# Softmax attentions in another order, with a spare 512-column product per query in some stretches

## The chip, the core and the metric

The kernel runs on one NeuronCore of one Trainium2 chip. The metric is the device time of one execution in microseconds (us). The core has a matrix engine (TensorE, PE in the profile, with its weight loads as PEld), a vector engine (DVE), an activation engine (ACT), GpSimd (POOL) and a queue engine (SP). Each engine runs its own instructions strictly in the order in which they were written, and waits at semaphores for the others. TensorE is granted one of two clocks, 2.4 GHz (1.00 in the profile's PEclk) and 1.2 GHz (0.50).

## What is computed

A first block (four kinds of sequence mixing, depth 1) is followed by a second block of two layers. What matters here are the softmax attentions: one forgetting attention in the first block, and in each layer of the second a differential attention (two softmaxes per query block, the second subtracted with a weight) and a neighbourhood attention (one softmax with a bias).

```python
def forgetting_attention(q, k, v, log_f):
        logits = (jnp.einsum('bhqd,bhkd->bhqk', qb, k) * scale
                  + cb[..., None] - cum[:, :, None, :])
        logits = jnp.where(key_pos[None, :] <= q_pos[:, None], logits, -jnp.inf)
        return jnp.einsum('bhqk,bhkd->bhqd', jax.nn.softmax(logits, axis=-1), v)
...
def diff_core(q, k, v, lam):
    s = jnp.einsum('bhcqd,bhckd->bhcqk', q, k).astype(jnp.float32) * (DIFF_QK ** -0.5)
    a = jax.nn.softmax(s, axis=-1)
    w = (a[:, :, 0] - lam * a[:, :, 1]).astype(v.dtype)
    return jnp.einsum('bhqk,bhkd->bhqd', w, v)
...
        s_loc = jnp.einsum('bhjd,bhajkd->bhjak', qr, kr).astype(jnp.float32) * scale + bias
        s_ctx = jnp.einsum('bhjd,bhcd->bhjc', qr, kc).astype(jnp.float32) * scale
        s = jnp.concatenate([s_loc.reshape(b, N_NA, GRID_W, n_loc), s_ctx], axis=-1)
        a = jax.nn.softmax(s, axis=-1).astype(vr.dtype)
```

## The kernel before

All five attentions run through one function, `softmax_attention` (L601). It takes a list of queries (a query is one head with one block of 128 positions) and writes, for each engine, a loop over t = 0 .. n + 1. The queries are software-pipelined through that loop. The steps of query t are these.

- **scores** (PE, L640): products of the query with its keys into PSUM, 128 x `kw`. In the differential attention there are two (n_comp = 2), c0 and c1, with 32 contraction rows each; `score_tile` gives two PSUM slots in turn, so scores of one component wait (`exped`) for the exponential of the one two before.
- **maximum** (DVE, L686): one per component, after the score; the neighbourhood attention adds its bias first (L685).
- **exponential** (ACT, L725): one per component, after its maximum.
- **combine** (DVE, `combine`): for two components a reciprocal (L695), a ratio (L696) and the weighted sum (L699); for one only a reciprocal (L693). It waits for all exponentials of the query.
- **turn** (PE, L653): `kw`/128 transposes of the weights; it waits for combine (or, with one component, for the exponential).
- **copy** (ACT, L733, `copy_turned`): the transposed weights to SBUF; ACT does it behind the exponentials of the next query.
- **mix** (PE, L663): `kw`/128 products with the values. **output** (DVE, L704): the result scaled into `y`.

In turn t of the loop, before the change, PE does scores(t), the work beside, turn(t-1), mix(t-2). DVE does combine(t-1), the maxima of t, output(t-2), the work beside. ACT does the exponentials of t, copy(t-1), the work beside.

The work beside is handed in as functions (`pe_beside`, `dve_beside`, `act_beside`). In the forgetting attention (16 queries, `kw` 128 to 512) it is part of the modulation's products. In the differential attention it is first the projection of six weight units of 128 x 1024 (`n_pieces` pieces, each 24 products at L228 to L230), then normalisation jobs (one 128 x 128 product with up to 512 columns each at L1834, square, root and scale around it), then nothing. Layer 0 has 24 queries: 0 to 15 with `kw` 768, 16 to 23 with `kw` 256; pieces run beside 0 to 11 and jobs beside 12 to 19. Layer 1 has 16 queries, all with `kw` 768; pieces run beside 0 to 7, jobs beside 8 to 13. A weight unit is split into a high part by ACT (L420, called from `act_beside`, so behind copy(t-1)) and a low part by DVE (L428); PE waits for the low part. In layer 1, the pieces 4 to 7 each use a unit of their own, which was split in the turn before. In the neighbourhood attention (24 and 16 queries) the work beside is a Fourier transform (kinds "features", L2094, and "tokens", L2100), a gate and transposes.

The differential attention flows from the work before it without a meeting of engines, and ends in one (`meet`); the neighbourhood attention lies between two.

## Time and profile before

| | us |
|---|---|
| median of 3 runs | 2380.97 (2379.16 to 2387.37) |
| the profiled execution | 2386.32 |
| its span in the trace | 2384.5 |
| matmul busy (PE) | 2247.4 |
| VectorE busy (DVE) | 1237.9 |
| ScalarE busy (ACT) | 752.4 |
| forgetting attention, from and to (span's clock) | 369 to 436 |
| differential attention, layer 0 | 693 to 841 |
| neighbourhood attention, layer 0 | 841 to 958 |
| differential attention, layer 1 | 1725 to 1850 |
| neighbourhood attention, layer 1 | 1850 to 1940 |

The page gives busy times per engine and, in 40 slices, the clock that TensorE was granted. A timeline row is: start, duration, engine, line, operation, what it writes and reads, shapes, how many were merged, and in brackets how long the engine stood idle before it and who released it. One fp32 product is recorded as two matmuls (halves). Busy times include the end of the pipeline, so two PE rows may overlap by some tenths of a microsecond.

### The profile page before, as it was taken

To read this page: it belongs to the slowest core of one execution; us is meant where nothing else is said; L and a number is where in the kernel's file an instruction comes from. 1 tells how busy PE (TensorE), PEld (TensorE's weight loads), DVE (VectorE), ACT (ScalarE), POOL (GpSimd) and SP (SyncE) were. 2 spreads that over 40 slices of the span, in tenths; PEclk is the share of its full clock that TensorE was granted. 3 is DMA by queue.
4 is the path that set the end of the run, shared out by engine and by line. 5 is a ranking of instruction groups with operands and counts; after the bars stand their busy time and mean duration, and the time that the engine had idled before them with its cause. 6 is when DMAs were issued, how large, how long until landed. Compare 5 with 4: busy or idle time off the path is not lost.

```text
span 2384.5 us, 29921 instructions
## 1 busy us (share of the span) xinstructions
PE 2247.4 (94%) x11458; PEld 1758.2 (74%) x11458; DVE 1237.9 (52%) x1923; ACT 752.4 (32%) x1154; POOL 42.3 (2%) x75
## 2 busy tenths in 40 slices
PE   6999899999999999989999989998999999999898
PEld 5678785456778657778888878886777676888786
DVE  5653333347335645466666653436456456666543
ACT  4521112354234523341111112234335333222232
POOL 0001110000000000000000000000000000000000
PEclk9999899899999779999999999999998889999999
DMA  5531216752111200111111111121112002222222
GB/s 185 168 131 38 71 47 221 264 193 71 53 45 36 85 0 1 46 52 62 62 62 62 62 62 62 55 70 53 62 39 90 1 27 80 89 97 96 88 94 74
DMA packets 50397, 187.95 MB, mean 79 GB/s; under 512 B 5424, under 2 KB 5424, under 8 KB 49664
## 3 DMA queue, kind: packets, MB, share of 16 engines
q1 hardware_dynamic: 46688, 168.32, 21.0%
q0 software_dynamic: 2240, 15.48, 1.7%
q10 hardware_dynamic: 1376, 2.85, 0.3%
q8 instruction: 66, 1.08, 0.2%
q14 instruction: 27, 0.22, 0.0%
HBM read 184.53 MB, written 2.10 MB: 78 GB/s over the span
## 4 chain that ended last, share of the span: by engine, by line
PE 85%; DVE 8%; ACT 2%; issue 2%; PEld 1%; DMA 1%; DVEq 0%; ACTq 0%; PEldq 0%; SPq 0%; POOLq 0%
PE psum L228 21%; PE psum L229 20%; PE psum L230 20%; PE psum L640 5%; PE psum L663 5%; PE psum L653 3%; PE psum L2100 2%; PE psum L1736 1%; PE psum L1290 1%; PE psum L1279 1%; PE psum L1301 1%; PE psum L1298 1%; DVE h_low L386 1%; PE psum L1834 1%; DVE unit_low L428 1%
## 5 line engine op out<-in xcount | busy, mean ns | idle before, releaser
L228 PE MATMUL psum<-h_high,unit_high 128*128 128x512 f32 (+1 forms) x1528 | 562.4, 368 | 12.4 <-DVE h_low L386 6.4
L229 PE MATMUL psum<-h_low,unit_high 128*128 128x512 f32 (+1 forms) x1528 | 549.9, 360 | 0.0
L230 PE MATMUL psum<-h_high,unit_low 128*128 128x512 f32 (+1 forms) x1528 | 549.7, 360 | 0.0
L420 ACT CAST unit_high<-ring 128x1024 fp32r<-128x1024 f32 x194 | 203.3, 1048 | 619.9 <-PE psum L230 619.2
L428 DVE TENSOR_TENSOR unit_low<-ring,unit_high 128x1024 fp32r<-128x1024 f32 x194 | 236.9, 1221 | 256.7 <-ACT unit_high L420 256.7
L228 PEld LDWEIGHTS psum<-h_high,unit_high 128*128 128x128 f32 x1528 | 289.3, 189 | 83.4 <-issue 19.5
L230 PEld LDWEIGHTS psum<-h_high,unit_low 128*128 128x128 f32 x1528 | 289.0, 189 | 46.2
L229 PEld LDWEIGHTS psum<-h_low,unit_high 128*128 128x128 f32 x1528 | 289.6, 190 | 41.4 <-issue 0.7
L228 PE MATMUL psum<-hidden_part_high,unit_high 128*128 128x512 f32 (+1 forms) x528 | 190.1, 360 | 19.9 <-DVE hidden_part_low L2365 16.8
L229 PE MATMUL psum<-hidden_part_low,unit_high 128*128 128x512 f32 (+1 forms) x528 | 189.1, 358 | 0.0
L230 PE MATMUL psum<-hidden_part_high,unit_low 128*128 128x512 f32 (+1 forms) x528 | 187.9, 356 | 0.0
L2251 DVE TENSOR_SCALAR conv_out<-psum,parameters 128x512 f32<-128x512 f32 (+1 forms) x132 | 91.2, 718 | 176.9 <-PE psum L230 176.9
L725 ACT ACTIVATE probs<-psum,neg_max 128x768 f32<-128x768 f32 (+4 forms) x136 | 105.6, 780 | 238.5 <-DVE neg_max L686 220.6
L2256 DVE SCALAR_TENSOR_TENSOR conv_out<-psum,parameters,conv_out 128x511 f32<-128x511 f32 (+1 forms) x264 | 166.4, 658 | 23.9 <-DVE conv_out L2251 1.7
L640 PE MATMUL psum<-p 32*128 32x512 f32 (+4 forms) x464 | 142.9, 540 | 3.6 <-ACTq L203 1.8
L704 DVE TENSOR_SCALAR y<-psum,inv 128x64 f32<-128x64 f32 x96 | 27.2, 284 | 203.8 <-PE psum L663 203.8
L663 PE MATMUL psum<-v,turned 128*128 128x64 f32 x912 | 125.7, 289 | 2.3 <-DVE y L704 2.3
L228 PEld LDWEIGHTS psum<-hidden_part_high,unit_high 128*128 128x128 f32 x528 | 100.2, 190 | 36.5 <-issue 16.6
L663 PEld LDWEIGHTS psum<-v,turned 128*128 128x128 f32 x912 | 123.1, 212 | 3.0 <-issue 1.9
L686 DVE TENSOR_REDUCE neg_max<-psum 128x1 f32<-128x768 f32 (+4 forms) x136 | 105.9, 803 | 34.4 <-PE psum L640 33.1
L230 PEld LDWEIGHTS psum<-hidden_part_high,unit_low 128*128 128x128 f32 x528 | 100.2, 190 | 15.6
L229 PEld LDWEIGHTS psum<-hidden_part_low,unit_high 128*128 128x128 f32 x528 | 100.4, 190 | 14.2
(363 smaller groups left out, 2906.4 us busy)
## 6 DMA issues: line engine op xcount, KB each, us to landing
ring<-in_w_units SPq DMA_DIRECT2D x317, 512.0 KB, 3.3
dft<-in_dft POOLq DMA_DIRECT2D x2, 2048.0 KB, 7.9
bias<-in_na_bias POOLq DMA_DIRECT2D x2, 2048.0 KB, 13.0
xT<-in_x ACTq DMA_DIRECT2D x4, 512.0 KB, 6.3
xT<-in_x POOLq DMA_DIRECT2D x1, 2048.0 KB, 11.0
out_x<-xT SPq DMA_DIRECT2D x1, 2048.0 KB, 7.2
constants_first<-in_constants_first POOLq DMA_DIRECT2D x1, 1361.0 KB, 9.1
xT<-in_ctx POOLq DMA_DIRECT2D x1, 1024.0 KB, 15.5
```

Of the source, the lines that this page charges most:

```text
L228: pe.matmul(out, lh, rh, start=first, stop=False, skip_group_check=True)
L229: pe.matmul(out, lh, rl, start=False, stop=False, skip_group_check=True)
L230: return pe.matmul(out, ll, rh, start=False, stop=last, skip_group_check=True)
L420: act.copy(K.w_high[:, q % 2], K.ring[:, q % RING]).then_inc(K.high_split.sem, 1)
L428: dve.tensor_tensor(K.w_low[:, q % 2], K.ring[:, q % RING], K.w_high[:, q % 2].bitcast(F32), ALU.subtract).then_inc(K.unit_used.sem, 1)
L640: mm = pe.matmul(score_tile(t, c, c0, c0 + w), lhs, rhs, start=(g == 0), stop=(g == len(group) - 1), skip_group_check=len(group) > 1)
L653: mm = pe.transpose(K.psum[:, 4 * S + b * P:4 * S + b * P + P], probs[:, t % 2, 0, b * P:b * P + P], const(K, "ident"))
L663: mm = pe.matmul(K.ps[6][:, 0:HD], turned[:, t % 2, b * P:b * P + P], items[t]["v"](tile), start=(b == 0), stop=(b == len(tiles) - 1))
L686: max_ready.up(dve.reduce_max(neg_max[:, t, c:c + 1], score_tile(t, c, 0, kw), AX, negate=True))
L725: exped.up(act.activation(probs[:, t % 2, c, 0:kw], score_tile(t, c, 0, kw), ACT.Exp, bias=neg_max[:, t, c:c + 1], accum_out=row_sum[:, t, ...
L2251: ins = dve.tensor_scalar(t[:, j, c0:c0 + w], bank[:, 0:w], column(wc + 44), column(bc), ALU.mult, ALU.add)
L2256: ins = dve.scalar_tensor_tensor(part, bank[:, src:src + w - 1], column(wc + 88 * (tap - 1)), part, ALU.mult, ALU.add)
```

## The change

Three things change in `softmax_attention`, and two callers pass a new argument.

1. PE does mix(t-2) ahead of turn(t-1) instead of behind it, in all five attentions.
2. With two components, DVE does the maximum of c0 of query t, then combine(t-1), then the maximum of c1 of t. With one component its order stays.
3. A query in the new range `warm` gets one more product on PE, ones (128 x 128) with 512 columns of the constants, fp32, written into its first score tile ahead of the scores and overwritten by them; it stands behind the wait on `exped`. There are 28: queries 12 to 23 of the differential attention of layer 0, 8 to 15 of layer 1, and 0 to 3 of both neighbourhood attentions.

```diff
@@ softmax_attention, tensor engine
                     n = t * n_comp + c
                     if n >= 2:
                         pe.wait_ge(exped.sem, exped.base + n - 1)
+                    if t in warm and c == 0:
+                        pe.matmul(score_tile(t, c, 0, S), const(K, "ones"), K.cst[:, 0:S], start=True, stop=True)
                     for group in items[t]["scores"][c]:
...
                 if beside:
                     beside(pe, t)
+                if 0 <= t - 2 < n_items:
+                    mix(t - 2)
                 if 0 <= t - 1 < n_items:
                     turn(t - 1)
-                if 0 <= t - 2 < n_items:
-                    mix(t - 2)
@@ softmax_attention, vector engine
-            def maxima(t):
+            def maxima(t, comps):
                 kw, bias = items[t]["kw"], items[t]["bias"]
-                for c in range(n_comp):
+                for c in comps:
...
             for t in range(n_items + 2):
+                if t < n_items and n_comp == 2:
+                    maxima(t, range(1))
                 if 0 <= t - 1 < n_items:
                     combine(t - 1)
                 if t < n_items:
-                    maxima(t)
+                    maxima(t, range(n_comp - 1, n_comp))
@@ differential_attention
-    softmax_attention(K, items, K.neg_lam[:, layer:layer + 1], pe_beside, dve_beside, act_beside, end=False)
+    softmax_attention(K, items, K.neg_lam[:, layer:layer + 1], pe_beside, dve_beside, act_beside, end=False,
+                      warm=range(n_pieces, len(items)))
@@ neighbourhood_attention
-    softmax_attention(K, items, None, pe_beside, dve_beside, act_beside)
+    softmax_attention(K, items, None, pe_beside, dve_beside, act_beside, warm=range(4))
```

PE, differential attention of layer 0, around the first two queries with a job (12 and 13); the four products from `p` are the scores, those from `probs` the turn, those from `turned` the mix. Before:

```order
L640 MATMUL psum<-p 128x512
L640 MATMUL psum<-p 128x256
L640 MATMUL psum<-p 128x512
L640 MATMUL psum<-p 128x256
L1834 MATMUL psum<-head_squares,constants 128x512
L653 MATMUL psum<-constants,probs 128x128 x6
L663 MATMUL psum<-v,turned 128x64 x6
```

and now:

```order
L639 MATMUL psum<-constants 128x512
L642 MATMUL psum<-p 128x512
L642 MATMUL psum<-p 128x256
L642 MATMUL psum<-p 128x512
L642 MATMUL psum<-p 128x256
L1838 MATMUL psum<-head_squares,constants 128x512
L665 MATMUL psum<-v,turned 128x64 x6
L655 MATMUL psum<-constants,probs 128x128 x6
```

The spare product stands ahead of the scores, and the mix ahead of the turn. DVE at the same place; the two reductions are the maxima, the sum into `probs` ends the combination. Before:

```order
L695 RECIPROCAL inv<-row_sum 128x2
L696 SCALAR_TENSOR_TENSOR ratio<-inv,row_sum,scalars 128x1
L699 SCALAR_TENSOR_TENSOR probs<-probs,ratio 128x768
L686 TENSOR_REDUCE neg_max<-psum 128x1 x2
L704 TENSOR_SCALAR y<-psum,inv 128x64
L1848 SCALAR_TENSOR_TENSOR p<-p,parameters,head_rstd 128x512
L1827 TENSOR_TENSOR head_squares<-p 128x512
```

and now:

```order
L688 TENSOR_REDUCE neg_max<-psum 128x1
L697 RECIPROCAL inv<-row_sum 128x2
L698 SCALAR_TENSOR_TENSOR ratio<-inv,row_sum,scalars 128x1
L701 SCALAR_TENSOR_TENSOR probs<-probs,ratio 128x768
L688 TENSOR_REDUCE neg_max<-psum 128x1
L706 TENSOR_SCALAR y<-psum,inv 128x64
L1852 SCALAR_TENSOR_TENSOR p<-p,parameters,head_rstd 128x512
L1831 TENSOR_TENSOR head_squares<-p 128x512
```

One maximum moved ahead of the combination, so the combination now stands behind scores(t).

## Rows read from the trace of the kernel before

**Rows 1.** The page: busy time by engine, and the granted clock in 40 slices.
```profile
PE 2247.4 (94%) x11458; PEld 1758.2 (74%) x11458; DVE 1237.9 (52%) x1923; ACT 752.4 (32%) x1154; POOL 42.3 (2%) x75
...
PEclk9999899899999779999999999999998889999999
```

**Rows 2.** Windows (from:to, length, busy by engine, PEclk, DMA): layer 0, jobs and end.
```profile
788.00:842.00 54.00, 47.88 (x217) 33.72 (x216) 34.53 (x89) 29.95 (x78) 0.00 (x0) 0.70 0.14 57
```

**Rows 3.** Timeline, layer 0, differential attention: turn t = 15 at the full clock.
```profile
803.54 1.56 PE L640 MATMUL psum<-p 32*128 32x512 f32 x8
...
804.58 0.16 DVE L695 RECIPROCAL inv<-row_sum 128x2 f32<-128x2 f32 x1
...
805.96 1.82 DVE L686 TENSOR_REDUCE neg_max<-psum 128x1 f32<-128x768 f32 x2
...
806.10 0.88 PE L653 MATMUL psum<-constants,probs 128*128 128x128 f32 x6 [0.36 <-DVE probs L699]
...
806.81 1.45 PE L663 MATMUL psum<-v,turned 128*128 128x64 f32 x12
...
808.19 1.43 PE L640 MATMUL psum<-p 32*128 32x256 f32 x4
```

**Rows 4.** Timeline, same attention: starts of scores 13 and 23, and the last output.
```profile
789.35 1.86 PE L640 MATMUL psum<-p 32*128 32x512 f32 x6
...
833.99 1.41 PE L640 MATMUL psum<-p 32*128 32x256 f32 x4
...
841.01 0.28 DVE L704 TENSOR_SCALAR y<-psum,inv 128x64 f32<-128x64 f32 x1 [1.27 <-PE psum L663]
```

**Rows 5.** Timeline, same attention: a turn with keys of 256 columns (t = 17).
```profile
814.41 0.16 DVE L695 RECIPROCAL inv<-row_sum 128x2 f32<-128x2 f32 x1
...
815.26 0.75 DVE L686 TENSOR_REDUCE neg_max<-psum 128x1 f32<-128x256 f32 x2
...
815.40 0.44 PE L653 MATMUL psum<-constants,probs 128*128 128x128 f32 x2
```

**Rows 6.** Timeline and waits of PE, layer 1, differential attention beside the projection.
```profile
1761.82 0.80 ACT L733 COPY turned<-psum 128x768 f32<-128x768 f32 x1 [3.36 <-PE psum L653]
1762.52 1.05 ACT L420 CAST unit_high<-ring 128x1024 fp32r<-128x1024 f32 x1
...
1763.91 1.22 DVE L428 TENSOR_TENSOR unit_low<-ring,unit_high 128x1024 fp32r<-128x1024 f32 x1
...
PE psum L228 <- DVE unit_low L428: 1.8, 3, 0.6
PE psum L1834 <- DVE head_squares L1827: 1.3, 1, 1.3
```

**Rows 7.** The same spare product elsewhere (all halves: min/median/max), and dense halves in a timeline.
```profile
L354 PE MATMUL psum<-constants x32: 592/592/1061, 568.6 to 1998.9; 128*128 128x512 f32 x32
...
854.52 7.13 PE L2100 MATMUL psum<-dft,fourier_z 128*128 128x512 f32 x16
```

**Rows 8.** Timeline, layer 1, differential attention: scores 9 and 15, a late exponential, the last output.
```profile
1800.05 0.89 ACT L725 ACTIVATE probs<-psum,neg_max 128x768 f32<-128x768 f32 x1
...
1800.35 2.29 PE L640 MATMUL psum<-p 32*128 32x512 f32 x8
...
1833.60 2.94 PE L640 MATMUL psum<-p 32*128 32x512 f32 x8
...
1849.51 0.28 DVE L704 TENSOR_SCALAR y<-psum,inv 128x64 f32<-128x64 f32 x1 [2.98 <-PE psum L663]
```

**Rows 9.** Neighbourhood attention, layer 0: timeline rows, and windows for the clock.
```profile
863.52 1.55 PE L640 MATMUL psum<-p 64*128 64x512 f32 x4
...
871.57 2.07 PE L2094 MATMUL psum<-constants,p 128*128 128x256 f32 x4 [1.95 <-DVE fourier_z L2145]
...
842.00:852.00 10.00, 10.00 (x20) 5.32 (x20) 5.04 (x7) 4.01 (x6) 0.00 (x0) 0.50 0.00 0
871.00:884.00 13.00, 12.43 (x31) 8.10 (x32) 5.50 (x11) 2.78 (x5) 0.00 (x0) 0.50 0.01 1
```

More of the change, by code:

```diff
@@ L601, in softmax_attention @@
 def softmax_attention(K, items, neg_lam=None, beside=None, dve_beside=None, act_beside=None,
-                      end=True):
+                      end=True, warm=range(0)):
     n_comp = len(items[0]["scores"])
```

## Prediction

> **What bounds the kernel now.** I read the page first: TensorE is busy for 94% of the span and VectorE for 52%, and the granted clock is at its upper level but for a few slices [rows 1]. So most of the kernel is matmul at 2.4 GHz and the change doesn't touch it. The slices with a 7 lie in the differential and the neighbourhood attention of layer 0; over the jobs and the end of the differential attention the clock's mean is 0.70 [rows 2]. Then I read the timeline of one turn of the loop, because only there does one see what a swap of two steps is worth.
>
> A turn with 768 keys at the full clock runs so [rows 3]: scores at 803.54, combination from 804.58, turn at 806.10 right behind its last sum, mix at 806.81, next scores at 808.19. TensorE waits only 0.36 us for the combination. The turns are thus nearly full of PE work and still hang on DVE. In the stretch with jobs, from scores 13 at 789.35 to scores 23 at 833.99, ten turns take 44.64 us [rows 4], part of it at 1.2 GHz. Scores 13 to 16 alone take 808.19 - 789.35 = 18.84 us for three turns, though the third takes 4.65 [rows 3, 4].
>
> The profiled execution is 2386.32 us with a span of 2384.5, and lies 5.4 us above the median of 2380.97. I work out differences in the trace and apply them to the median. A measurement of this kernel can tell about 0.3% (7.1 us) from no change.
>
> **Price of one spare product.** The trace has the very product elsewhere, at L354: a half takes 592 ns at its median and 1061 at most, with the end of the pipeline in it [rows 7]. In a dense run 16 halves take 7.13 us, so a half takes some 0.435 us and a product 0.87 us at 2.4 GHz; 1.74 us at 1.2 GHz.
>
> **The new turn, full clock, 768 keys.** PE does spare product, scores, job, mix(t-2), turn(t-1). DVE does the first maximum, the combination, the second maximum. The turn now has a closed chain: spare product 0.87, scores c0 1.55 (a component with nothing beside it, [rows 9]), its maximum 1.82/2 = 0.91, combination to the start of the turn 806.10 - 804.58 = 1.52, transposes 806.81 - 806.10 = 0.71 [rows 3]. Sum 5.56 us. PE's own work in it is 0.87 + 1.56 + 0.65 (a job of 512 or 256 columns) + 1.38 + 0.71 = 5.2, so the chain ends last. Without the spare product the chain would be 4.69, below the 5.2 or so of the old turns at the full clock. So order and product nearly cancel: the order is worth half a microsecond a turn and the product takes it back. What remains depends on the clock.
>
> **Layer 0, jobs.** Turns 13 to 15: 3 x 5.56 = 16.7. Turn 16 has scores of 256 columns and a combination of 768: 0.87 + 0.70 (half of 1.41 at the half clock, [rows 4]) + 0.38 + 1.52 + 0.71 = 4.2. Turn 17 is PE's: 0.87 + 0.70 + 0.65 + 1.38 + 0.24 = 3.85. Turns 18 to 22: 0.87 + 0.70 + 0.38 + 0.99 (814.41 to 815.40) + 0.24 = 3.2 each [rows 5], 16.0. Together 40.7 against 44.64: **-3.9**. From scores 23 to the last output it takes 7.0 now [rows 4]. With the mix done ahead, I count 0.70 + 0.38 + 0.99 + 0.38 + 0.6 + 0.99 + 0.3 + 0.5 + 0.56 = 5.4: **-1.6**. All this takes the full clock for granted. Queries 20 to 23 have no job, and the spare product is most of their dense work; at 1.2 GHz such a turn would be 1.74 + 1.41 + 0.38 + 0.99 + 0.5 = 5.0, thus 1.8 more, 7.2 for four. I take **+2** of 0 to 7, as I expect a fall towards the end.
>
> **Layer 1, jobs.** Scores 9 to 15 took 33.25 for six turns [rows 8]; six at 5.56 are 33.4: **0**. The end, scores 15 to the last output, took 15.9 at the half clock. At the full clock: 1.55 + 0.91 + 1.52 + 0.91 + 1.0 + 1.52 + 0.8 + 0.9 + 1.45 = 10.6, a gain of 5.3; at the half clock 13.8, a gain of 2.1. I take **-4.5**, nearer to the full clock, because the spare products run until scores 15.
>
> **Layer 1, projection: a cost of the new order.** ACT splits the next weight unit behind copy(t-1), and copy(t-1) waits for the turn. Now the copy starts 0.85 us after the turn's start, 1761.82, the cast at 1762.52, the low part at 1763.91, and PE waits for it 3 times, 1.8 us in all [rows 6]. With the mix (1.38) ahead of the turn the copy starts 1.38 later. The low part started 0.34 behind the end of the cast, as DVE had output and copy to do first; that slack is eaten, so it ends 1.38 - 0.34, about 1.05 us later. PE reaches the piece at the same time as before, so each of the three waits grows by that, and so does the wait for the first job's square (1.3 [rows 6]), which stands behind a low part. **+4.3** (bounds 0, if DVE or ACT is ahead, and 5.5, four full mixes). In layer 0 a unit is used two turns later, so some 6 us of piece cover it: 0. The forgetting attention has PE full with the modulation's products: 0, between -0.5 and +0.5.
>
> **Neighbourhood attentions.** Here one component is at work, DVE's order stays, and PE is full from the start: it runs 842 to 852 without a gap, at 1.2 GHz [rows 9]. The spare products 0 and 1 are bare time at 1.74 each, product 2 at 0.87. Product 3 stands before an idle time of 1.95 that DVE ends, and is hidden; if that idle goes, it costs 0.87 more. Two layers: **+8.7**. Against it: denser work may lift the clock earlier. If it rises 3.5 us earlier in each, that is half of 3.5 each: **-3.5** (0 to -10, the whole of the stretch in both layers). And the stretch 871 to 884 at 0.50 [rows 9] begins in that idle time; if it shrinks and the clock stays, up to 6 us go. I take **-3**.
>
> Sum: -3.9 - 1.6 + 2 + 0 - 4.5 + 4.3 + 8.7 - 3.5 - 3 = -1.5 us, so 2379.5 us: no change that can be told.
>
> **Rivals.**
> Rival 1, the clock stays up. The spare products hold 2.4 GHz through both differential attentions, and in the neighbourhood attentions it rises within the second spare product and does not fall at 871. Then the terms are -5.5, 0, -5.3, +4.3, +7.0 (one product at 1.74 and two at 0.87 in each), -6 and -6: -11.5, **2369.5**. For it: the existing turns have one fp32 product of full width and two light steps, and flicker between both levels; one more full product tips that. Against it: 842 to 852 is without a gap and still at 0.50.
>
> Rival 2, slower: the spare products run at 1.2 GHz. It decides at queries 16 and after in layer 0 and 12 and after in layer 1, where the clock fell before. If it falls all the same, seven turns cost 1.8 more (12.6), three wide turns of layer 1 cost 1.74 + 2.94 + 0.91 + 1.52 + 1.4 = 8.5 instead of 5.56 (8.8), the neighbourhood pays 8.7 with nothing back, the projection 4.3; early turns and end give 4.2 back. Sum +30, **2411**; half of it, if only one layer does so, 2396.
>
> Rival 3, scores fall apart. In rows, two components of 32 rows take 1.56 together [rows 3], as much as one of 64 rows alone, 1.55 [rows 9]; where c1 waits for an exponential that runs until 1800.94, they take 2.29 [rows 8]. The second maximum now stands behind the combination, so the exponential of c1 comes 1.5 us later relative to that of c0, and the pair may run apart in every wide turn with a job: ten times 0.73, +7.3, **2387**. My chain above has this partly: PE has 0.36 us to spare in a turn.
> The Trainium skill (TensorE: Matmul & The Clock Gate, Part 3: Packing small matmuls) says that products in different groups of rows run at the same time in the array; by that rule, with which the trace agrees, the rival's loss is real once c1 is late, and without the rule its sum would be nothing, as the two would follow each other anyway.
>
> **How the numbers follow.** Forecast 0.35 (2374 to 2386), rival 1 0.31, rival 2 0.15, rival 3 0.19. The range takes in rival 1 with some 5 us below it, rival 3, and the smaller half of rival 2: 2364 to 2397. Faster by over 0.3% (below 2373.8): most of rival 1 and a little of the forecast, 0.34. Slower (above 2388.1): rival 2, a third of rival 3 and the forecast's upper bounds, 0.28. Same: 0.38.
>
> **What would show it.** In the trace after, wide turns with jobs should be 5.4 to 5.7 us from scores to scores, with TensorE waiting at the turn for the combination by some tenths; a turn near 4.7 would mean that I chained it wrongly. The waits of PE for the low part in layer 1 should grow from 1.8 to about 5 us; if they stay, the cost of the order is wrong. The granted clock over the jobs of layer 0 should rise from 0.70 to 0.85 or more, and the neighbourhood attention should begin with two spare products of 1.7 us. A clock of 0.70 or less there makes rival 2 true, a clock of 1.00 into the neighbourhood attention rival 1; score groups of 2.3 us in most turns show rival 3. The forecast is wrong above all if the clock's falls and rises move as a whole, since each microsecond of my terms for it rests on where they stood in one execution.

## The result and the profile after

The changed kernel takes **2394.38 us** (median of ten executions, 2388.28 to 2409.33) where the kernel before takes 2381.82 us (ten on the same chip, 2360.71 to 2392.15). The ratio is **1.0071, with a 95% interval of 1.0036 to 1.0105**: slower by 0.7%. The forecast was 2379.5 us and no change; the measured time lies inside the range (2364 to 2397) but on its slow side. Of the twelve executions of e3_mix_first below two count as slow and are left out of its ratio, while its median is that of all twelve.

The profiled execution after is 2392.30 us (span 2390.5), the one before 2386.32 (span 2384.5). These two differ by only 6.0 us where the medians differ by 12.6. The page of the changed kernel, to be held against [rows 1]: busy time by engine, and the granted clock in 40 slices.

```profile
PE 2253.4 (94%) x11514; PEld 1747.3 (73%) x11514; DVE 1240.0 (52%) x1923; ACT 757.9 (32%) x1154; POOL 42.2 (2%) x75
...
PEclk9999899899999989899999999999998989999999
```

The two slices with a 7 are gone. TensorE has 6.0 us more busy time for 28 more products (56 halves). Two windows over the jobs of layer 0, first of the kernel before (from:to, length, busy by engine, PEclk, DMA):

```profile
790.00:842.00 52.00, 45.88 (x203) 32.03 (x202) 33.05 (x86) 28.11 (x75) 0.00 (x0) 0.68 0.11 45
```

and of the changed kernel, with the neighbourhood attention of layer 0 and the jobs and end of layer 1:

```profile
790.00:842.00 52.00, 46.06 (x243) 29.87 (x242) 35.69 (x92) 30.71 (x77) 0.00 (x0) 0.97 0.15 63
842.00:967.00 125.00, 117.24 (x549) 77.64 (x550) 65.10 (x136) 47.84 (x91) 0.00 (x0) 0.88 0.00 1
1797.00:1853.00 56.00, 51.25 (x256) 37.68 (x256) 34.63 (x64) 28.73 (x53) 0.00 (x0) 0.84 0.16 67
```

So the clock over the jobs rose from 0.68 to 0.97 (the fall from 839 on lies behind the last scores; from scores 12 to 23 it is 0.75 before and 1.00 after), and the kernel still got slower. To see where, I cut both traces at the same events: the start of a query's scores, and the last output of an attention. All in us; "else" is the rest of the span, work that is the same in all these kernels but for the order in the forgetting attention.

```
                           layer 0                        layer 1
kernel           pieces  jobs   end  neighb.   pieces  jobs   end  neighb.    else    span
                 s0-s12 s12-s23                 s0-s8  s8-s15
before             91.4   49.7   7.0   117.3      69.2   39.5  15.9    90.2  1904.2  2384.5
after              95.5   47.9   6.3   114.3      73.8   44.0  14.4    92.9  1901.4  2390.5
e1 order only      94.7   51.8   6.9   116.9      72.9   37.7  16.2    93.5  1908.0  2398.8
e2 spare only      92.3   45.1   6.3   122.2      68.5   37.2  13.4    94.2  1904.7  2383.9
e3 mix first       95.0   57.0   6.5   115.7      74.7   34.9  10.6    89.0  1897.8  2381.2
e4 max first       91.7   68.4   8.3   117.5      69.2   62.1  18.4    93.4  1894.5  2423.5
e5 old by pieces   92.3   47.9   6.1   111.4      68.5   39.7  14.4    92.9  1907.9  2381.2
e6 spare diff.     92.3   45.1   6.3   115.3      70.1   37.2  11.8    96.6  1897.5  2372.3
e7 e6, late mix    92.3   44.0   5.4   115.7      70.1   36.9  13.1    93.0  1907.6  2378.1
e8 before again    91.4   51.2   7.0   109.2      69.1   39.5  15.9    93.4  1894.7  2371.5
e9 split first     92.3   47.9   6.4   110.4      66.5   39.5  14.4    92.9  1899.2  2369.7
e10 e6, split      92.3   45.0   5.3   109.1      70.1   37.2  10.3    92.2  1899.8  2361.3
e11 256 columns    91.9   43.0   5.3   118.4      68.1   36.0  13.6    93.1  1900.8  2370.2
e12 combined       91.9   42.4   6.3   112.3      66.0   34.1  12.4    90.7  1899.4  2355.5
```

Between before and after, the losses are +4.1 beside the pieces of layer 0, +4.6 beside those of layer 1, +4.5 in the jobs of layer 1 and +2.7 in its neighbourhood attention. The gains are 1.8, 0.7 and 3.0 in layer 0, 1.5 at the end of layer 1, and 2.8 in work outside. That is +6.1, the difference of the spans (6.0) but for rounding.

Two things have to be known for reading this table. A short fall of the clock to 1.2 GHz beside the pieces of layer 1 lengthens their column by 1.6 us (in the kernel before, a turn of 11.42 instead of 9.84, with the low clock from 1775.1 to 1778.5). Nine of the fourteen traces have such a fall, in the old order and in the new: before, after, e1, e4, e6, e7, e8, e10, and e3, which has two; e2, e5, e9, e11 and e12 have none. And every row is one execution, whose time can lie well off its kernel's median: 17.6 us below in e3, 10.9 below in e10, 8.6 above in e2 and e7.

**The turn with jobs.** Timeline of the changed kernel at the full clock, the turn that answers to [rows 3] (start, length, engine, line and tiles, in brackets the idle time before and what ended it):

```profile
803.48 1.02 PE L639 MATMUL psum<-constants 128*128 128x512 f32 x2
...
804.44 1.78 PE L642 MATMUL psum<-p 32*128 32x512 f32 x8
...
806.03 0.96 DVE L688 TENSOR_REDUCE neg_max<-psum 128x1 f32<-128x768 f32 x1 [1.52 <-PE psum L642]
...
806.90 0.15 DVE L697 RECIPROCAL inv<-row_sum 128x2 f32<-128x2 f32 x1
...
808.42 0.88 PE L655 MATMUL psum<-constants,probs 128*128 128x128 f32 x6 [0.29 <-DVE probs L701]
...
809.13 1.02 PE L639 MATMUL psum<-constants 128*128 128x512 f32 x2
```

The reader is to see a ring: spare product 0.96, scores until the maximum 1.59, maximum 0.87, combination to turn 1.52, turn 0.71, and the next spare product at 809.13. Sum 5.65 us. DVE waits 1.52 us for the scores and PE then 0.29 us for DVE: each waits for the other once a turn.

**Beside the pieces of layer 0.** Timeline of the changed kernel, from one turn's copy to the scores of the next query:

```profile
731.01 0.80 ACT L737 COPY turned<-psum 128x768 f32<-128x768 f32 x1 [4.26 <-PE psum L655]
...
731.70 1.05 ACT L420 CAST unit_high<-ring 128x1024 fp32r<-128x1024 f32 x1
...
732.79 1.23 DVE L428 TENSOR_TENSOR unit_low<-ring,unit_high 128x1024 fp32r<-128x1024 f32 x1 [1.56 <-ACT unit_high L420]
...
733.93 0.95 DVE L688 TENSOR_REDUCE neg_max<-psum 128x1 f32<-128x768 f32 x1
...
737.16 0.90 ACT L729 ACTIVATE probs<-psum,neg_max 128x768 f32<-128x768 f32 x1 [1.20 <-DVE neg_max L688]
...
737.37 2.39 PE L642 MATMUL psum<-p 32*128 32x512 f32 x8
```

The copy stands behind the turn, the cast behind the copy, the low part behind the cast, and the first maximum of the next query behind the low part, since all stand in one row on their engines. The last exponential starts at 737.16 and the scores at 737.37, so the second component can't follow the first at once, and the pair takes 2.39 us. In the kernel before such a pair takes 1.57 us in every turn beside a piece but one, as here:

```profile
737.41 1.57 PE L640 MATMUL psum<-p 32*128 32x512 f32 x8
```

In the changed kernel four more take 2.4.

**Layer 1.** Waits of PE between 1700 and 1800 us of the changed kernel (total, times, longest), against 1.8 and 1.3 in [rows 6]:

```profile
PE psum L228 <- DVE unit_low L428: 4.8, 3, 1.6
PE psum L1838 <- DVE head_squares L1831: 1.4, 1, 1.4
```

and the timeline of its PE at the first job:

```profile
1797.58 1.78 PE L1838 MATMUL psum<-head_squares,constants 128*128 128x512 f32 x2 [1.43 <-DVE head_squares L1831]
...
1799.15 2.66 PE L665 MATMUL psum<-v,turned 128*128 128x64 f32 x12
...
1801.60 1.49 PE L655 MATMUL psum<-constants,probs 128*128 128x128 f32 x6
...
1802.88 1.91 PE L639 MATMUL psum<-constants 128*128 128x512 f32 x2
...
1804.72 1.57 PE L642 MATMUL psum<-p 32*128 32x512 f32 x8
```

After a wait of 1.43 us the clock is at 1.2 GHz for 7 us, from 1798: the mix takes 2.66 instead of 1.45 and the spare product 1.91 instead of 1.02. From scores 8 to scores 9 it takes 10.1 us, before 6.3.

### The profile page after: what moved, and what is told of

Read it like the earlier page. It is cut to its first block, busy times and chain, and to the rows that moved or that the text cites. A ratio compares the mean times of both kernels' runs of the same rounds, so it can differ in the third digit from the quotient of the medians.

```text
span 2390.5 us, 30033 instructions
## 1 busy us (share of the span) xinstructions
PE 2253.4 (94%) x11514; PEld 1747.3 (73%) x11514; DVE 1240.0 (52%) x1923; ACT 757.9 (32%) x1154; POOL 42.2 (2%) x75
## 4 chain that ended last, share of the span: by engine, by line
PE 87%; DVE 7%; ACT 2%; issue 2%; DMA 1%; DVEq 0%; ACTq 0%; SPq 0%; POOLq 0%
PE psum L228 21%; PE psum L230 20%; PE psum L229 20%; PE psum L642 5%; PE psum L665 4%; PE psum L655 2%; PE psum L1740 2%; PE psum L2105 1%; PE psum L639 1%; PE psum L1294 1%; PE psum L1305 1%; PE psum L1302 1%; DVE h_low L386 1%; PE psum L1838 1%; PE psum L1283 1%
## 5 line engine op out<-in xcount | busy, mean ns | idle before, releaser
L642 PE MATMUL psum<-p 32*128 32x512 f32 (+4 forms) x464 | 136.7, 508 | 2.3 <-ACTq L203 1.8
L642 PEld LDWEIGHTS psum<-p 32*128 32x128 f32 (+1 forms) x464 | 63.7, 189 | 73.3 <-issue 69.1
```

The lines of the kernel that those rows point to most:

```text
L642: mm = pe.matmul(score_tile(t, c, c0, c0 + w), lhs, rhs, start=(g == 0), stop=(g == len(group) - 1), skip_group_check=len(group) > 1)
```

## The experiments

All are compared with the kernel before in five rounds on one chip, except e8, which is a single execution. Ratios below 1 are faster than before. Nothing of the computation is left out in any of them; the spare products are overwritten by the scores.

**e1_order_only** is the changed kernel without its spare products, **e2_spare_only** the kernel before with them. The part that e1 leaves out and e2 adds:

```diff
+                    if t in warm and c == 0:
+                        pe.matmul(score_tile(t, c, 0, S), const(K, "ones"), K.cst[:, 0:S], start=True, stop=True)
```

> The changed kernel without the 28 spare products; both changes of order stay. Theory A (the order costs beside the projection: pairs of scores apart and later low parts): the differential attentions keep their losses up to scores 12 (layer 0) and 8 (layer 1), about 3 and 4 us against before; with jobs a wide turn falls from 5.65 us to about 4.8 at the full clock, but the clock falls as in before; time between before and changed kernel, ratio to before 1.000 to 1.004. Theory B (the spare products cost it all): the ratio is 0.997 or less and projection turns are as before.

Measured: 1.007 (1.0042 to 1.0098), 2400.53 us against 2379.98, above what I expected. The losses beside the pieces are there (94.7 and 72.9). But the wide turns did not fall to 4.8: at the full clock of layer 1 (1815 to 1844) they take 4.8 to 5.6, 5.15 in the mean, where the kernel before takes 4.80 and 5.18 in turn (e8, 1784 to 1804), and their pairs take 1.9 to 2.6 (e8: 1.9 to 2.3).

> The kernel before with the 28 spare products alone, old order on both engines. Theory A: the projection stretches are as before to within 0.5 us; wide turns with jobs last about 5.7 us (spare product 0.87 on the old chain of about 5.0), the clock stays up over the jobs as in the changed kernel; ratio 0.998 to 1.003. Theory B: ratio 1.005 or more, as much as the whole change.

Measured: 0.9986 (0.9964 to 1.0007), 2377.12 us. The order is the loss, and it loses 0.7% without the spare products and 1.0071/0.9986, 0.85%, with them. In the old turn the spare product is nearly hidden: at the full clock of layer 1 the turns take 4.98 and 5.41 in turn, 0.2 us more than the 4.80 and 5.18 of e8, for a product that stands there with 1.0. Window and timeline of e2:

```profile
790.00:842.00 52.00, 47.26 (x230) 27.73 (x231) 33.81 (x85) 28.16 (x74) 0.00 (x0) 0.91 0.09 37
```

```profile
799.26 1.08 PE L639 MATMUL psum<-constants 128*128 128x512 f32 x2
800.27 1.56 PE L642 MATMUL psum<-p 32*128 32x512 f32 x8
...
802.30 0.82 PE L655 MATMUL psum<-constants,probs 128*128 128x128 f32 x6
802.95 1.45 PE L665 MATMUL psum<-v,turned 128*128 128x64 f32 x12
804.24 1.08 PE L639 MATMUL psum<-constants 128*128 128x512 f32 x2
```

From spare product to spare product 4.98 us, and the turn at 802.30 starts without a wait: here the combination doesn't stand behind the new scores, so the spare product fills time in which DVE combines. With the same product the new order needs 5.65. I had expected 5.7 here.

**e3_mix_first** and **e4_max_first** each make one half of the new order on the kernel before, without spare products.

```diff
+                if 0 <= t - 2 < n_items:
+                    mix(t - 2)
                 if 0 <= t - 1 < n_items:
                     turn(t - 1)
-                if 0 <= t - 2 < n_items:
-                    mix(t - 2)
```

> Only TensorE's order is changed (mix ahead of turn); VectorE's order is old and there is no spare product. Theory A1 (later low part is the mix's doing): waits of TensorE for the low part in layer 1 grow from 1.8 us to about 4.8. Pairs of scores in the projection of layer 0 apart (2.4 us instead of 1.57 in every other turn) only if the mix alone delays the exponentials of c1; I expect a part of them. Ratio 1.000 to 1.004.

Measured: 1.0063 (1.0034 to 1.0091), 2400.61 us, more than I expected. The profiled execution is 2382.99 us, so the trace shows where this kernel differs, but not its typical loss. A row of its timeline and one of its waits from 1700 to 1800:

```profile
736.21 2.43 PE L642 MATMUL psum<-p 32*128 32x512 f32 x8
```

```profile
PE psum L228 <- DVE unit_low L428: 4.8, 3, 1.6
```

Both losses beside the pieces come with the mix alone: 95.0 us in layer 0, and 74.7 in layer 1, of which 1.6 is a second fall of the clock (1794.6 to 1798.0). Without that it is 73.1, 3.9 above the kernel before; e1 has 3.7. Its jobs show two faces: in layer 0 at the half clock 57.0, in layer 1 at the full clock 34.9, with wide turns of 4.5 to 5.0 with a job, thus shorter than those of e1. So it is the maximum ahead of the combination that lengthens them.

```diff
+                if t < n_items and n_comp == 2:
+                    maxima(t, range(1))
                 if 0 <= t - 1 < n_items:
                     combine(t - 1)
                 if t < n_items:
-                    maxima(t)
+                    maxima(t, range(n_comp - 1, n_comp))
```

> Only VectorE's order is changed (first maximum ahead of the combination); TensorE's order is old and there is no spare product. The low-part waits stay at 1.8 us. If the second maximum behind the combination is what sets the scores apart, every other score group of the projection in layer 0 lasts 2.4 us here and 1.57 us with the mix alone moved. Turns with jobs get longer, since the turn stands ahead of the mix and waits for a combination that now stands behind a maximum: 5.2 to 5.9 us at the full clock. Ratio 1.001 to 1.006.

Measured: 1.0182 (1.0149 to 1.0214), 2426.07 us, three times the loss that I expected at most. PE in the timeline of e4:

```profile
801.24 1.54 PE L655 MATMUL psum<-constants,probs 128*128 128x128 f32 x6 [0.41 <-DVE probs L701]
802.58 2.66 PE L665 MATMUL psum<-v,turned 128*128 128x64 f32 x12
805.17 2.94 PE L642 MATMUL psum<-p 32*128 32x512 f32 x8
...
810.52 1.54 PE L655 MATMUL psum<-constants,probs 128*128 128x128 f32 x6 [1.27 <-DVE probs L701]
```

Without the mix ahead of it, the turn comes sooner and waits 1.27 us for a combination that stands behind a maximum. The clock is down from 783 to 820 and from 1810 to 1858, and the wide turns there take 9.3 us in both layers. Beside the pieces nothing is lost (91.7 and 69.2), so the late second maximum is not what takes the pairs apart there.

**e5_old_beside_units** is the changed kernel with both old orders in the turns that have a piece (`late` is `n_pieces`), **e6_spare_diff** the kernel before with only the 20 spare products of the differential attentions.

```diff
-                if 0 <= t - 2 < n_items:
+                if t >= late and 0 <= t - 2 < n_items:
                     mix(t - 2)
                 if 0 <= t - 1 < n_items:
                     turn(t - 1)
+                if t < late and 0 <= t - 2 < n_items:
+                    mix(t - 2)
```

> The changed kernel, but in the differential attentions the old orders on both engines for the turns in which a projection piece stands beside (0 to 11 in layer 0, 0 to 7 in layer 1). All 28 spare products and the new order elsewhere stay. Theory A (the loss sits beside the projection): scores 0 to 12 of layer 0 take 92.4 us (as with spare products alone) instead of 95.5, scores 0 to 8 of layer 1 69.5 instead of 73.8, and the turn after the last piece of layer 1 6 to 8 us instead of 10.1, since TensorE no longer stands idle before the first job; in all 8 to 10 us less than the changed kernel, ratio to before 0.998 to 1.003. Theory C (the new order costs everywhere, mostly with jobs): at most 3 us less than the changed kernel, ratio 1.004 or more.

Measured: 0.9991 (0.9974 to 1.0009), 2382.26 us against 2384.29. The loss beside the pieces is gone (92.3 and 68.5) and with it the whole slowdown, 0.8% or 19 us. Of these the traces place 13: 3.2 and 5.3 beside the pieces (1.6 of it the clock) and 4.3 in the jobs of layer 1; the rest is within what the two intervals leave open.

> The kernel before with spare products in the differential attentions alone (20; none in the neighbourhood attentions), old order. If the 8 products of the neighbourhood attentions are bare cost, these get 2.5 to 4.5 us shorter each than with them (122.2 and 94.2 us) and the whole is the fastest version so far, ratio 0.993 to 0.998, near 2370 us. If they earn their price by the clock, the ratio is that of the spare products alone or worse, 0.9986 and up.

Measured: **0.9947 (0.9925 to 0.9969)**, 2371.6 us. Its window over the jobs of layer 0:

```profile
790.00:842.00 52.00, 47.27 (x223) 27.71 (x222) 33.90 (x87) 29.27 (x74) 0.00 (x0) 0.89 0.04 18
```

The eight products of the neighbourhood attentions cost about 0.4% (e2 against e6; the intervals just overlap). In the table these stretches are 4.5 us longer in e2 than in e6, together, but as 6.9 longer in layer 0 and 2.4 shorter in layer 1, and the two executions of the kernel before differ there by 4.9. So it is the ratios that carry this price, and not the traces.

**e7_late_mix** is e6 with the mix first where no piece stands beside; **e8_before_again** is the kernel before once more, to see how far two of its executions differ.

> Spare products in the differential attentions alone, VectorE's order old everywhere, and mix ahead of turn only in those turns of the differential attentions where no projection piece stands beside. With both maxima ahead of the next combination and the mix filling TensorE's wait, a wide turn is TensorE's own work, 5.0 to 5.2 us, against 5.0 to 5.4 with the old order and 5.65 in the changed kernel: stretch with jobs of layer 0 44 to 46 us, of layer 1 35.5 to 37. Ratio 0.992 to 0.998. If the wait for the combination stays as long as the spare product, the stretches equal those of the old order and nothing is won by the mix.

Measured: 0.9962 (0.9939 to 0.9985), 2371.29 us: no different from e6. The jobs are shorter by 1.1 and 0.3 us, less than a measurement can tell.

> The kernel before, unchanged, once more under the profiler: how far the places of the half clock move from one execution to the next. If the clock's falls are set by the program, the stretches between landmarks agree with the first trace to 1 us; if its phase is free, stretches with jobs and neighbourhood attentions move by several us each.

Measured: 2373.26 us, span 2371.5, 13 us below the first profiled execution. This execution runs 4.7 us ahead of the first when the neighbourhood attention begins (836.3 against 841.0), so its windows are laid 5 us earlier; against 0.50 for both in [rows 9]:

```profile
837.00:847.00 10.00, 10.00 (x19) 5.33 (x20) 4.73 (x7) 4.01 (x5) 0.00 (x0) 0.50 0.00 0
866.00:879.00 13.00, 12.60 (x53) 7.62 (x53) 4.95 (x11) 2.90 (x6) 0.00 (x0) 1.00 0.00 1
```

At the start of the attention the clock is low in both. But around the wait of PE that ends at 866.11 (1.94 us) it does not fall, where in the first trace it fell at 870.6, within the same wait (1.95 us), and stayed low for 13.6 us, so the neighbourhood attention takes 109.2 instead of 117.3 with nothing changed. A further 9.5 us lie in "else". The chip need not be the reason: on e8's own chip 29 more executions of this kernel go from 2369.44 to 2394.27 us.

**e9_split_first** is the changed kernel with the split of the weight unit ahead of the copy on ACT, in turns with a piece; **e10_best_split_first** does the same to e6.

```diff
+                early = act_beside and t < split_ahead
+                if early:
+                    act_beside(act, t)
                 if 0 <= t - 1 < n_items:
                     copy_turned(t - 1)
-                if act_beside:
+                if act_beside and not early:
                     act_beside(act, t)
```

> The changed kernel, but ScalarE does the work beside (the high part of the next weight unit, or the copy of a context piece) ahead of the copy of the transposed weights in the turns with a projection piece; the rest as changed. If the loss beside the projection is the chain turn, copy, high part, low part, then it is gone although the mix stays ahead of the turn: TensorE's wait for the low part in layer 1 falls from 4.8 us to 0 to 0.5, the score pairs of 2.4 us go back to 1.57, scores 0 to 12 of layer 0 take 92 to 92.5 us, scores 0 to 8 of layer 1 67 to 69, and the turn before the first job no longer 10.1 but about 6. Ratio to before 0.996 to 1.002. If the mix ahead costs in another way (the turn itself late), the stretches stay at 95.5 and 73.8.

Measured: 0.9989 (0.9971 to 1.0006), 2378.57 us against 2380.86. Timeline of e9:

```profile
1765.94 1.04 ACT L420 CAST unit_high<-ring 128x1024 fp32r<-128x1024 f32 x1
...
1769.57 0.80 ACT L737 COPY turned<-psum 128x768 f32<-128x768 f32 x1 [2.59 <-PE psum L655]
1769.70 1.22 DVE L428 TENSOR_TENSOR unit_low<-ring,unit_high 128x1024 fp32r<-128x1024 f32 x1
```

The cast is done 2.6 us before the copy, the low part no longer follows a cast, and PE doesn't wait for it at all. In layer 0 the pairs are together again:

```profile
736.41 1.57 PE L642 MATMUL psum<-p 32*128 32x512 f32 x8
```

The pieces take 92.3 and 66.5 us. Both orders stay as in the changed kernel, so this shows the cause: the turn delays the copy, and the copy delays the split. In layer 0 the edit also puts ACT's copy of a context piece ahead in every second turn; it doesn't tell the two apart there.

> Old orders on TensorE and VectorE, spare products in the differential attentions alone, and ScalarE's split ahead of its copy beside the pieces. The waits for the low part (1.8 us) and for the first job's square (1.3 us) of the kernel before go too: scores 0 to 8 of layer 1 67 to 68 us instead of 68.5 to 70, and 1 us at the first job. Ratio 0.991 to 0.996, 1 to 3 us below the same kernel without this move. If the clock's phase rules instead, the two can't be told apart.

Measured: 0.9972 (0.9953 to 0.9991), 2373.93 us. No gain over e6, and my expectations were wrong: the waits of 1.8 us stay, the pieces of layer 1 take 70.1 us as in e6, and from scores 8 to scores 9 it is 6.26 us in both. Waits of e10 from 1700 to 1800, and its timeline:

```profile
PE psum L228 <- DVE unit_low L428: 1.8, 3, 0.6
```

```profile
1757.05 1.57 PE L642 MATMUL psum<-p 32*128 32x512 f32 x8
1757.16 0.28 DVE L706 TENSOR_SCALAR y<-psum,inv 128x64 f32<-128x64 f32 x1 [6.28 <-PE psum L665]
1757.36 0.68 DVE L2022 COPY p<-psum 128x512 f32<-128x512 f32 x1
...
1757.95 1.21 DVE L428 TENSOR_TENSOR unit_low<-ring,unit_high 128x1024 fp32r<-128x1024 f32 x1
...
1759.22 0.51 PE L228 MATMUL psum<-h_high,unit_high 128*128 128x512 f32 x1 [0.61 <-DVE unit_low L428]
```

With the turn ahead of the mix, DVE stands at the output, which waits for the mix, the last product ahead of the scores. The low part is behind that, whenever the cast was done. The early split pays only where the mix comes first too.

**e11_spare_256** is e6 with spare products of 256 columns. **e12_combined** puts together what each run had left over: mix first everywhere, the old order of the maxima, the split ahead of the copy, and 256-column products in the differential attentions alone.

```diff
-                        pe.matmul(score_tile(t, c, 0, S), const(K, "ones"), K.cst[:, 0:S], start=True, stop=True)
+                        pe.matmul(score_tile(t, c, 0, C), const(K, "ones"), K.cst[:, 0:C], start=True, stop=True)
```

> As the kernel with spare products in the differential attentions alone, but each with 256 columns instead of 512, so half the price. If half the product still holds the clock over the jobs, stretches with jobs are as with 512 columns or up to 2 us shorter (45.1 and 37.2 us) and the clock is at the upper level there; if it doesn't, the clock falls in layer 0 before scores 20 and the stretches are 47 to 50 and 38 to 40, ratio 0.997 to 1.000.

Measured: 0.9964 (0.9944 to 0.9985), 2370.65 us, no different from e6 in time. The jobs are 2.1 and 1.2 us shorter, and the clock over them is as high as in e2 (1.00 in both from scores 12 to 23; the window reaches beyond them):

```profile
790.00:842.00 52.00, 46.21 (x236) 29.58 (x233) 36.45 (x89) 30.46 (x77) 0.00 (x0) 0.91 0.09 37
```

> What paid, together: mix ahead of turn everywhere, both maxima behind the combination as in the kernel before, ScalarE's split ahead of its copy beside the pieces, spare products of 256 columns in the differential attentions alone. If the terms add up, scores 0 to 8 of layer 1 take 66 to 66.5 us (no wait for a low part, 3 us less than before), the stretches with jobs 41.5 to 43.5 and 34.5 to 36 us, and the ratio to before is 0.990 to 0.995. If the clock's phase in the rest of the program covers them, the ratio is as with the spare products alone, 0.995 to 0.997.

Measured: **0.9914 (0.9883 to 0.9946)**, 2360.7 us against 2384.9: the lowest ratio of all, though its interval overlaps that of e6, and faster than both kernels. The pieces take 91.9 and 66.0 us, the jobs 42.4 and 34.1, as expected or shorter. PE in its timeline, layer 0:

```profile
797.27 1.56 PE L642 MATMUL psum<-p 32*128 32x512 f32 x8
...
799.30 1.45 PE L665 MATMUL psum<-v,turned 128*128 128x64 f32 x12
...
800.58 0.83 PE L655 MATMUL psum<-constants,probs 128*128 128x128 f32 x6
...
801.25 0.60 PE L639 MATMUL psum<-constants 128*128 128x256 f32 x2
```

This wide turn takes 4.50 us (797.27 to the next scores at 801.77; the others take up to 4.98), and nothing in it waits: the mix covers the combination, which doesn't stand behind the new scores.

## Why the prediction was wrong, step by step

I forecast no change (-1.5 us), and the kernel is 12.6 us slower by the medians. In the traces the losses lie beside the pieces, where the sum had 0 in layer 0, and in the turn of the first job of layer 1, for which it had next to nothing. That the time still lies inside the range is luck: the range was drawn around rivals that did not happen as told.

- **The new turn: right.** 5.56 forecast, 5.65 measured, by the same links; the narrow turn 3.2 against 3.3. From scores 13 (793.14) to scores 23 (835.36) it is 42.2 us where I had 40.7; turn 16 (5.15 instead of 4.2) holds most of the rest. Against 44.64 before the gain is 2.4 and not 3.9. In layer 1 scores 9 to 15 take 33.9 where I had 33.4.
- **"Order and product nearly cancel": the wrong comparison.** I took the old turn for full, at 5.2 us of PE work, and so the product for time added. At the full clock the old turn takes 5.0 in the mean (e8), and with the product 5.2 (e2): all but 0.2 hides behind DVE. And the half microsecond that the order should give is not there: e1 takes 5.15 where I had 4.69. What the change gained in jobs the product alone gives, and more (45.1 and 37.2, against 47.9 and 44.0).
- **The projection of layer 0, priced at 0: this step failed first.** I had looked only at the unit that PE needs later, which the 6 us of piece do cover; PE never waits for it there. I had not followed the low part on DVE, where the next query's maximum stands behind it. The cost is 4.1 us: 0.9 for the spare product of query 12, which stands ahead of its scores (e2 has 92.3 by that alone), and 3.2 for four pairs of 2.4 instead of 1.57. e3 has it, e4 has not, e9 removes it.
- **The projection of layer 1: right in place and size, but not whole.** The waits grew from 1.8 to 4.8, where I had about 5. With one more pair apart (0.8) and the spare product of query 8, which stands ahead of its scores (0.9), that is the 4.6. My 4.3 had the wait for the first job's square in it: it grew from 1.3 to 2.29 in e1 and e3, as I had worked out, and to 1.43 here, as the spare product of query 8 fills the rest.
- **Turns and products that the sum left out.** My stretches begin at scores 13 and at scores 9. So the spare products of queries 12 and 8 (0.9 each), the turn from scores 12 to 13 (5.10 to 5.68) and that from scores 8 to 9 (6.26 to 10.14) had no term, but for the wait. The last is most of the +4.5 in the jobs of layer 1: the clock fell in it, so the spare product of query 9 takes 1.84, and job, mix and turn 1.9 more. That the new order brings this fall is not shown. e1 has the longer wait at the same place, and no fall behind it:

```profile
1811.60 1.10 PE L1838 MATMUL psum<-head_squares,constants 128*128 128x512 f32 x2 [2.29 <-DVE head_squares L1831]
1812.53 1.45 PE L665 MATMUL psum<-v,turned 128*128 128x64 f32 x12
```

  e3 has the same rows (2.29 us, no fall). Both have a low clock earlier, in the last piece (1799.8 to 1803.2 and 1794.6 to 1798.0), and such falls stand beside pieces of the kernel before too. The kernel before in both its executions waits 1.3 us for the first job without a fall.
- **The end of layer 1: -4.5 forecast, -1.5 measured.** The clock fell at 1842, 3.6 us behind the start of the last scores, and stayed low for 20 us; at 14.4 us it is near my value for the half clock, 13.8. In layer 0 the clock held until 839, so the +2 for queries 20 to 23 was not needed; the end there gave 0.7 where I had 1.6.
- **Neighbourhood attentions: +2.2 forecast, -0.3 measured in this pair of traces**, as -3.0 and +2.7. The early rise did not come: products 0 and 1 run at the half clock. The timeline of PE in the changed kernel:

```profile
842.31 2.08 PE L639 MATMUL psum<-constants 128*128 128x512 f32 x2 [0.65 <-POOLq L207]
...
849.04 1.91 PE L639 MATMUL psum<-constants 128*128 128x512 f32 x2
```

  The gain in layer 0 is the stretch of the kernel before at 871, at whose place the clock doesn't fall here; in e8 it doesn't fall there either, without any change. The price of the products is seen only in the ratios of e2 and e6, about 0.4%, or 9 us, against the 8.7 that I had as their bare cost.
- **The rivals.** Of rival 1 the clock over the jobs of layer 0 came true and there was no fall at the place of 871; the early rise, the full clock in all of layer 1 and the gain did not come. Rival 2 did not occur in layer 0 (0.97). Rival 3 had the right effect at the wrong place and from the wrong cause: pairs fall apart beside the pieces, by the mix, and not in the turns with jobs by the late maximum, where they take 1.78 us behind a spare product (without one, in e1, 1.9 to 2.6). That its 7.3 us is near the 6.1 of the table is chance. The Trainium skill (TensorE: Matmul & The Clock Gate, Part 3: Packing small matmuls) says that products in different groups of rows run at the same time; the traces agree, with 1.57 us for a pair that starts together and 2.39 for one that doesn't.
- **The base.** I subtracted places of the half clock in one execution. e8 shows the same program 13 us shorter, 8.1 of it in the neighbourhood attention where I had put -3.5 and -3. So a term of 3 us for a shifted fall of the clock said nothing, and the difference of 6.0 between the two profiled executions doesn't contradict the 12.6 of the medians.

What stays open: why the clock falls where it does, at the first job of layer 1 above all. No kernel here moves a fall and nothing else. Also open is how much of the loss lies where: e1 is 0.7% (17 us) slower, and its trace has 7 of them beside the pieces.

## What to carry to other kernels

Where a step is moved on one engine, follow its consumer onto the next engine's queue and read what stands in the row behind it: here 1.4 us on TensorE went through a copy, a cast and a subtraction into maxima that had nothing to do with them. A filler product for the clock belongs in a turn where the other engine is what is waited for; look for that slack in the order that it will run in. And where two executions of one program differ by 13 us, read the price of an edit from the pitch of the turns and from repeated runs, not from a difference of two spans.

## What the runs showed of the hardware

- The stretches at 1.2 GHz move between executions of the same program: in the neighbourhood attention of layer 0 the kernel before has 871 to 884 at 0.50 in one and the same place (866 to 879) at 1.00 in the other, and its medians over five sets of runs, on several chips, go from 2379.98 to 2384.9.
- A filler of 256 columns held the clock over the jobs of layer 0 as high as one of 512 (0.91 in e11 and in e2), for 0.53 us a turn (e12, 796.74 to the scores at 797.27) instead of 1.01 (e2). In e12, where the mix comes first, it did not hold to the end of that stretch: the clock fell at 820.9, ahead of scores 22 and 23.
- Two full-width products at the start of the neighbourhood attention did not lift the clock: it was at 0.50 from 842 to 852 with PE busy for 9.69 of 10 us.
- The length of a wait does not tell whether the clock falls behind it: in the changed kernel it fell at 1798, directly behind a wait of PE of 1.43 us; e1 and e3 have a wait of 2.29 us at the same place without a fall, and at the same wait of 1.95 us in the neighbourhood attention of layer 0 the kernel before has a fall in one execution and none in the other.
